# A causal mask moves from a TensorE matmul into the second stream of a VectorE scan

## The reference

```
z = q @ k.T * 64 ** -0.5
mask = tk[None, :] < tq[:, None]                 # strictly causal
log_stay = where(mask, log_sigmoid(-z), 0)
after = cumsum(log_stay, reverse=True) - log_stay
w = where(mask, exp(log_sigmoid(z) + after), 0)
o = w @ v
```

## Time and profile before

| | |
|---|---|
| median of 3 runs | 849.94 us (849.93 to 850.0) |
| the profiled execution, span from first to last instruction | 852.7 us |
| TensorE busy | 809.2 us, 95% of the span |
| VectorE, ScalarE, GpSimd busy | 449.7, 331.2, 314.0 us |
| granted TensorE clock, mean of the span | 0.976 |

### The profile page before, as it was taken

The page is one execution under the profiler, slowest core; times in us unless marked ns, Lnnn a source line. Parts: engine busy times, 40 slices in busy tenths (PEclk is TensorE's granted clock), DMA queues, the critical chain, the costliest instruction groups (busy, mean ns, idle before and its releaser), DMA issues.

```text
span 852.7 us, 13543 instructions
## 1 busy us (share of the span) xinstructions
PE 809.2 (95%) x4623; PEld 659.0 (77%) x4623; DVE 449.7 (53%) x1023; ACT 331.2 (39%) x840; POOL 314.0 (37%) x261
## 2 busy tenths in 40 slices
PE   5699999999999999989999889999999999999996
PEld 4688888878787878746878878999777777765785
DVE  5556666666666676772135442115655555556322
ACT  6434333343333333341168333333444343446211
POOL 5345252525343444460123454434434232343100
PEclk9899999999999999967999999999999999999999
DMA  8531212030303030314032243230201002020211
GB/s 226 141 101 50 83 51 83 25 108 25 106 25 106 25 106 25 100 46 145 4 102 85 98 144 96 76 98 26 63 22 55 12 25 75 26 89 11 105 49 57
DMA packets 68082, 61.68 MB, mean 72 GB/s; under 512 B 7144, under 2 KB 55040, under 8 KB 68032
## 3 DMA queue, kind: packets, MB, share of 16 engines
q1 hardware_dynamic: 68032, 61.04, 23.4%
HBM read 50.85 MB, written 10.17 MB: 72 GB/s over the span
## 4 chain that ended last, share of the span: by engine, by line
PE 82%; DVE 6%; issue 5%; ACT 3%; POOL 2%; SPq 1%; DMA 1%; POOLq 0%; ACTq 0%; DVEq 0%
PE bank L416 17%; PE bank L418 17%; PE bank L417 17%; PE bank L676 5%; PE bank L968 3%; PE bank L710 3%; PE bank L688 3%; PE bank L1012 2%; PE bank L1014 2%; PE bank L1013 2%; PE bank L996 2%; PE bank L966 2%; PE bank L945 1%; DVE left L1753 1%; PE bank L980 1%
## 5 line engine op out<-in xcount | busy, mean ns | idle before, releaser
L1479 POOL TENSOR_TENSOR wlo<-raw,whi 128x1024 fp32r<-128x1024 f32 (+3 forms) x80 | 194.1, 2434 | 125.3 <-ACT whi L1098 125.0
L416 PE MATMUL bank<-whi,hthi 128*128 128x384 f32 (+1 forms) x360 | 129.4, 359 | 2.7 <-DVE wlo L1690 2.5
L417 PE MATMUL bank<-wlo,hthi 128*128 128x384 f32 (+1 forms) x360 | 125.6, 349 | 0.0
L418 PE MATMUL bank<-whi,htlo 128*128 128x384 f32 (+1 forms) x360 | 125.5, 349 | 0.0
L1098 ACT ACTIVATE whi<-raw 128x1024 fp32r<-128x1024 f32 (+3 forms) x84 | 82.4, 1008 | 32.8 <-PE bank L418 31.3
L1753 DVE TENSOR_TENSOR_SCAN left<-stay 128x512 f32<-128x512 f32 (+4 forms) x72 | 69.9, 971 | 20.7 <-ACT stay L1190 20.4
L1542 POOL TENSOR_TENSOR rstd<-msq,neg_half 128x4 f32<-128x4 f32 x40 | 40.3, 1007 | 100.6 <-DVE msq L1720 99.8
L416 PE MATMUL bank<-hthi,whi 128*128 128x272 f32 x256 | 75.0, 293 | 0.0
L416 PEld LDWEIGHTS bank<-whi,hthi 128*128 128x128 f32 x360 | 69.3, 193 | 6.9 <-issue 5.3
L418 PE MATMUL bank<-hthi,wlo 128*128 128x272 f32 x256 | 73.5, 287 | 0.0
L417 PE MATMUL bank<-htlo,whi 128*128 128x272 f32 x256 | 73.4, 287 | 0.0
(11 more groups left out here) (196 smaller groups left out, 1678.1 us busy)
## 6 DMA issues: line engine op xcount, KB each, us to landing
raw<-in_w_in_a SPq DMA_DIRECT2D x64, 256.0 KB, 3.1
raw<-in_w_in_b SPq DMA_DIRECT2D x24, 256.0 KB, 3.3
raw<-in_w_o_a SPq DMA_DIRECT2D x16, 256.0 KB, 2.8
raw<-in_w_kv_b SPq DMA_DIRECT2D x16, 256.0 KB, 3.1
raw<-in_w_o_b SPq DMA_DIRECT2D x16, 256.0 KB, 3.1
raw<-in_w_q_b SPq DMA_DIRECT2D x16, 192.0 KB, 2.4
x_in<-in_x_prompt SPq DMA_DIRECT2D x4, 512.0 KB, 5.1
out<-qkn SPq DMA_DIRECT2D x8, 256.0 KB, 2.4
```

The lines of the kernel that those rows point to most:

```text
L416: eng.matmul(dst, st[0], mv[0], start=(k == 0), stop=False)
L417: eng.matmul(dst, st[0], mv[1], start=False, stop=False)
L418: mm = eng.matmul(dst, st[1], mv[0], start=False, stop=(k == n - 1))
L1479: nc.gpsimd.tensor_tensor(wlo[slot][:, c], raw[:, c], whi[slot][:, c].bitcast(F32), ALU.subtract).then_inc(s_lo, 1)
```

## The change

The second matmul of `score_a` goes for the prompt's units (64 instructions in the run, 8 in a step); unit 0 keeps its own mask. The tile `causal` goes, and a tile `scan_mask` of 128 x 512 bf16 comes: 0 everywhere, and in its last 128 columns 1 where key is not before query. The scan gets it as its second operand, and its second operation becomes a maximum: left = max(left * stay, mask). On masked keys the running value is so held at 1, whatever the score; on the others max(x, 0) changes nothing. VectorE waits for the masks ahead of step 0. GpSimd clears 512 columns instead of 128, and makes the triangle in the last block. `scan_mask` shares its place with two small tiles that are used only after the first layer.

```diff
-        causal = keep("causal", [P, P], BF16)
...
-        sq_pe = keep("sq_pe", [P, ROPE])
-        pe_tmp = keep("pe_tmp", [P, 3, ROPE])
+        o_mask = at[0]
+        scan_mask = keep("scan_mask", [P, SEQ], BF16)
...
+        sq_pe, o = alias("sq_pe", [P, ROPE], o_mask)
+        pe_tmp, o = alias("pe_tmp", [P, 3, ROPE], o)
...
                 pe.matmul(b[:, 0:(i + 1) * P], qkt[r, par, 0, i * P:(i + 1) * P], qkt[r, par, 1, 0:(i + 1) * P],
-                          start=True, stop=True)
-                pe.matmul(b[:, i * P:(i + 1) * P], ident_b[:, :], causal[:, :], start=False, stop=True,
-                          skip_group_check=True).then_inc(s_score, 1)
+                          start=True, stop=True).then_inc(s_score, 1)
...
-            nc.gpsimd.memset(causal[:, :], 0.0).then_inc(s_zeros_m, 1)
+            nc.gpsimd.memset(scan_mask[:, :], 0.0).then_inc(s_zeros_m, 1)
...
-            nc.gpsimd.affine_select(out=causal[:, :], in_=causal[:, :], compare_op=ALU.is_gt, fill=BIG,
-                                    base=0, pattern=[[-1, P]], channel_multiplier=1).then_inc(s_masks, 1)
+            nc.gpsimd.affine_select(out=scan_mask[:, SEQ - P:SEQ], in_=scan_mask[:, SEQ - P:SEQ],
+                                    compare_op=ALU.is_gt, fill=1.0, base=0, pattern=[[-1, P]],
+                                    channel_multiplier=1).then_inc(s_masks, 1)
...
-                v.tensor_tensor_scan(out=left[0:r, ub, SEQ - n:SEQ][:, ::-1], data0=back, data1=back, initial=1.0,
-                                     op0=ALU.mult, op1=ALU.bypass).then_inc(s_left, 1)
+                hidden = scan_mask[0:r, 0:n] if u == 0 else scan_mask[:, SEQ - n:SEQ]
+                v.tensor_tensor_scan(out=left[0:r, ub, SEQ - n:SEQ][:, ::-1], data0=back, data1=hidden[:, ::-1],
+                                     initial=1.0, op0=ALU.mult, op1=ALU.max).then_inc(s_left, 1)
...
             step_a(-1, 1, att=False)
+            dve.wait_ge(s_masks, 6)
             step_a(0, 0)
```

More of the change, by code:

```diff
@@ L207, in build @@
         p_inv = keep("p_inv", [P, 2])
+        sq_pe, o = alias("sq_pe", [P, ROPE], o_mask)
+        pe_tmp, o = alias("pe_tmp", [P, 3, ROPE], o)
+        assert o <= o_mask + 2 * SEQ
         raw = keep("raw", [P, KD * 512])
```

## The result

| | before | changed |
|---|---|---|
| median, in alternation on one chip | 849.97 us (849.93 to 854.75, 4 runs) | 865.54 us (860.52 to 866.79, 4 runs) |
| time and span of the profiled execution | no time on record, 852.7 us | 866.79, 864.8 us |

The ratio is 1.0136, 95% interval 1.0097 to 1.0175: slower, as forecast, but by three times as much, and outside the range of 848.0 to 857.0. The spans of the two profiled executions differ by 12.1 us, and that difference can be placed.

What follows compares the result with a forecast made beforehand. TensorE, busy 95% of the span, was taken as the bound. Step 0 -0.15, step 1 -0.12, steps 2 to 6 +3.6 and step 7 +1.4 gave +4.7 on 849.94, so 854.7 us, range 848.0 to 857.0.

Steps and rivals of the forecast that it cites:

- The sigmoid 0.16 us earlier, POOL first in steps 1 to 6: At unit 2, ScalarE's earlier sigmoid lets POOL's subtraction start 0.17 us before VectorE's scan, which then takes about 3.47 us.
- The mask matmul saves 0.02 us: On TensorE, each mask matmul removed saves 0.02 us per unit, 0.16 per step of eight.
- the part given back: On TensorE, 0.05 of the 0.07 us saved per mask matmul returns at the tile change from score to transposes.
- The scan costs the same with a real second operation: VectorE's scan keeps its cost: 425 ns at 128 columns, 1.22 us at 512 when not held up.
- Steps 2 to 6 are 0.72 us longer each, +3.6: Stick-breaking steps 2 to 6: 0.84 us more each as in step 1, less six units at 0.02, together +3.6.
- step 1's -0.12: Stick-breaking step 1, where POOL already won: only the matmul savings count, -0.12 us.
- TensorE's clock only at the end of the stick-breaking part: Clock falling to half there, relative to the dense work's start, can give or take about 1 us, widening every case.
- Step 7 +1.4: Step without projections: order turns over at unit 2, +2.0 us, units 4 to 8 save 0.6, net +1.4.
- Step 0 -0.15: First step: POOL's subtraction would tie with unit 2's scan; scan taken as first, -0.15 us.
- The base: Starting time: 849.94 us median of the runs, with the profiled execution's span of 852.7 taken as 2.8 more.
- the rival in which only step 7 turns over: POOL gets ahead of unit 2's scan only in step 7: 850.3 us; chance 0.08, shared with only the steps turning.

Runs made afterwards that it cites:

- e5: Changed kernel with GpSimd's weight pieces 1 to 3 placed behind the weights of units 2, 4 and 8: 850.35 us, ratio 0.9931 to the kernel before.
- e6: Kernel before with GpSimd's weight pieces 1 to 3 placed behind the weights of units 2, 4 and 8: 852.48 us, ratio 0.9973.
- e1: Changed kernel with a second matmul per score tile again, adding zeros, mask still in the scan: median 855.3 us, ratio 1.0007 to the kernel before.
- e2: Kernel before with the mask matmul taken out and nothing in its place, scan as before: 863.58 us, ratio 1.0117.
- e7: Changed kernel with four extra 512-column zero matmuls on TensorE ahead of its wait for unit 2's weights: 856.41 us, ratio 1.0004 to the kernel before.
- e9: Kernel before, unchanged, run once more for a second profile: 863.05 us, span 861.2.
- e8: Changed kernel with two zero-adding matmuls after the score of unit 2 alone: 852.78 us, ratio 0.9977 to the kernel before.
- e10: Kernel before with its mask added twice at unit 2: 852.23 us, ratio 0.9966 to the kernel before.
- e11: Changed kernel with two zero-adding matmuls after the scores of units 2 and 4: 852.83 us, ratio 0.9987 to the kernel before.
- e3: Changed kernel with GpSimd's subtraction of piece 1 waiting for the scan of unit 2: 853.65 us, ratio 0.9994 to the kernel before.
- e4: Kernel before with GpSimd's subtraction of piece 1 waiting for the scan of unit 2: 855.63 us, ratio 1.0025.

## Why the sign was right and the size wrong

- **The sigmoid 0.16 us earlier, POOL first in steps 1 to 6**: right. POOL's lead was 0.177 to 0.184 us in all six steps (forecast 0.17). Scans of 3.44 and a wait of 0.79 in each of these steps, and a POOL pair of 5.76 in step 2, are near the forecast (3.47, 0.8 to 1.0, 5.66). The Trainium skill, "SBUF — State Buffer", section "Who interferes with whom", says that a VectorE instruction with two operands in SBUF contends with a GpSimd instruction that reads SBUF. The traces agree, 3.44 against 1.22 us.
- **The mask matmul saves 0.02 us**: right. e5 and e6 differ by 0.16 us of TensorE's time per step of eight. That the second half's weights come late, the prediction's reason for the part given back, was argued and no run shows it. The 81 ns that the Trainium skill gives in "TensorE: Matmul & The Clock Gate", section "Back-to-back issue gap", would make an estimated 0.65 us per step. Here the measurement decides: 0.16.
- **The scan costs the same with a real second operation**: right, 425 ns at 128 columns before and after, and e1 and e2 split the change with all of the loss on the matmul's side.
- **Steps 2 to 6 are 0.72 us longer each, +3.6**: this step of the prediction failed. It read: "I therefore take step 1 as the picture of steps 1 to 6." The waits themselves did cost what was forecast: e7, which keeps them and keeps TensorE busy, is 3.6 us longer in steps 1 to 6, where +3.6 - 0.12 was forecast. But step 1 of the kernel before had kept its full clock through its wait, and I took one draw for the rule. In the changed kernel the clock fell to 1.2 GHz with each of the six waits, for 3.4 or 6.8 us. The steps of e2 and e9 show all three outcomes of the same wait: 43.9 or 44.4 with none, 45.9 with 3.4 us, 47.0 to 47.6 with 6.8. With step 1's -0.12 the term was forecast at +3.5 and measured +17.1: 3.6 for the waits and 13.5 for the clock, which the sum had at nothing. I had named TensorE's clock only at the end of the stick-breaking part, as a matter of 1 us, though a wait in a stretch at full clock stood in the rows.
- **Step 7 +1.4**: wrong in sign. In the changed kernel the scan of unit 2 stays ahead:
```profile
387.49 1.21 DVE L1756 TENSOR_TENSOR_SCAN left<-stay,scan_mask 128x512 f32<-128x512 f32 x1
...
387.95 2.89 POOL L1480 TENSOR_TENSOR wlo<-raw,whi 128x1024 fp32r<-128x1024 f32 x1 [0.93 <-ACT whi L1099]
```
The prediction moved the sigmoid of unit 2 up and held the clock as it was. But it came 4.35 us after that of unit 1 (386.33 - 381.98), where before it was 3.86 (370.05 - 366.19); and the clock fell sooner, 2.1 us after the sigmoid of unit 1 in place of 2.5. The other traces go the same way. Where the clock fell 0.7 to 2.2 us after that sigmoid (e1, e7, e8, e9), the scan of unit 2 was first by 0.5 us or more; in e10 and e11 it fell 3.4 and 3.6 us after it, and POOL was first by 0.3. No run set that moment, so the link is read from traces only. From step 7 to the end the changed kernel takes 482.8 us and the kernel before 486.5, with 17.1 and 27.3 us of low clock in step 7's first 30 us. What decides when the clock falls in this stretch was not tried and stays open.
- **Step 0 -0.15**: the step is 42.95, against 43.08 (66.66 to 109.74), -0.13. The start-up ahead of it was 1.1 shorter; over the 13 profiles it varies by 2.6 us (64.81 to 67.45), so this says nothing on the change. The scan of unit 2 was first in step 0, as assumed, with POOL's record 12 ns ahead.
- The sum: 17.1 - 1.3 (start-up and step 0) - 3.7 (from step 7) = +12.1 = 864.8 - 852.7.
- **The base**: I put +4.7 on 849.94. In all 75 executions of this kernel beside the experiments the time is 1.8 to 1.9 us above the span. The profiled execution with its span of 852.7 will so have taken some 854.5, an estimate, and its span was not 2.8 us above its own time but 1.8 below it. The kernel before ran from 848.4 to 864 us beside the experiments, with medians of 853.2, 855.1 and 854.4; three runs within 0.07 us had looked like a firm number. Against those medians the change costs some 10 to 12 us.
- **Small slips**: the rival in which only step 7 turns over adds up to 850.5 and not 850.3, and step 6, cut where step 7 starts, is 38.91 us and not one of the two lengths of the earlier trace rows. Nothing rests on either: e7 takes 39.62 us there, 0.71 more, where 0.72 was forecast.

## What to carry to other kernels

Where two engines that shut each other out meet within some tenths of a microsecond, taking out 0.02 us of work, which moved a start by 0.16, made this kernel 12 us slower, and adding as little at unit 2 (e10) made it 0.3% faster. Look for such meetings first, and set the order by a semaphore or by the place in the program, at every meeting and not at one. Price a new wait on TensorE not by its length alone but by the low clock that can come with it: here a wait of 0.8 us had 2.3 us more to pay on the mean. One step of a profile in which a wait went well is one draw, and a repeated profile of the same kernel shows the others.

## What the hardware showed that I had not expected

- In steps 1 to 6 a lead of 14 to 19 ns of POOL in the records still left the scan first in all cases but one (17 ns), and 20 to 22 ns gave the turn to POOL in all. In step 0 of e7 a lead of 20 ns lost too. At such leads the records' start times don't tell who was first.
- With the same 0.8 us wait the granted clock stayed at 2.4 GHz, or was 1.2 GHz for 3.4 or for 6.8 us, in otherwise equal steps. Steps 1 to 6 of the 13 traces have 20 such waits, and 15 of them had the low clock, which began between 0.4 us before the end of the wait and 1.6 us after it; the 58 other steps, the six of e7 with a filled wait among them, had none. With four 512-column matmuls without a use in the wait it stayed at 2.4 in six steps of six, and the span of the profiled execution was 10.6 us shorter.
- TensorE's short waits of 0.1 to 0.4 us at unit 3 in e3, e4 and e8 were followed by no low clock in any of steps 1 to 6.
